# Differential attention: a score unit of the long sequence holds 1024 keys of one map instead of 512 keys of both

## The reference

```
qh = q.reshape(B, T, H, 2, HD).transpose(3, 0, 2, 1, 4) * (HD ** -0.5)
kh = k.reshape(B, T, H, 2, HD).transpose(3, 0, 2, 1, 4)
bias = -slopes[:, None, None] * jnp.abs(tq[:, None] - pos[None, :])
s = jnp.einsum('ibhqd,ibhkd->ibhqk', qblk, kh) + bias
p = jax.nn.softmax(s, axis=-1)
a = p[0] - lam * p[1]
return jnp.einsum('bhqk,bhkv->bhqv', a, vh)
```

## Time and profile before

| | |
|---|---|
| median of 3 runs | 3404.91 us (3400.65 to 3405.81) |
| profiled execution | 3406.49 us |
| its span | 3404.7 us |
| TensorE matmuls, busy | 3281.1 us (96%) |
| VectorE, busy | 1989.6 us (58%) |
| ScalarE, busy | 1324.1 us (39%) |
| GpSimd, busy | 1106.1 us (32%) |
| mean granted clock of TensorE | 0.985 |

### The profile page before, as it was taken

One profiled execution on the slowest core, in us unless ns is written; L12 is line 12 of the kernel. 1 busy time (PEld: TensorE's weight loads), 2 busy tenths in 40 slices (PEclk: granted clock), 3 DMA queues, 4 the chain that ended last, 5 costly groups with the idle time before them and its releaser, 6 DMA issues. The chain is left out here.

```text
span 3404.7 us, 50932 instructions
## 1 busy us (share of the span) xinstructions
PE 3281.1 (96%) x19032; PEld 2557.6 (75%) x19032; DVE 1989.6 (58%) x4609; ACT 1324.1 (39%) x2165; POOL 1106.1 (32%) x511
## 2 busy tenths in 40 slices
PE   7999999998999999999999988999999888999998
PEld 6888888886878888888877765666666556888887
DVE  3322312226566656665568788888888566556654
ACT  3111111114334343344323336767676555333322
POOL 3322323243333343333333325555555433000000
PEclk9999999999999999999999999999999999999999
DMA  6545445565454544544448965122221266667562
GB/s 214 182 153 188 154 156 176 173 208 177 133 182 146 180 151 125 190 145 141 131 161 292 324 210 155 45 75 64 67 62 38 100 229 229 226 230 237 176 217 75
DMA packets 317906, 554.89 MB, mean 163 GB/s; under 512 B 35421, under 2 KB 114525, under 8 KB 317662
## 3 DMA queue, kind: packets, MB, share of 16 engines
q1 hardware_dynamic: 266510, 471.26, 42.9%
q10 hardware_dynamic: 51152, 80.38, 6.5%
HBM read 382.03 MB, written 169.50 MB: 162 GB/s over the span
## 5 line engine op out<-in xcount | busy, mean ns | idle before, releaser
L731 POOL TENSOR_TENSOR glaf_w_lo<-early_raw,glaf_w_hi 128x1024 fp32r<-128x1024 f32 x140 | 350.0, 2500 | 638.6 <-ACT glaf_w_hi L705 638.6
L760 PE MATMUL glaf_dense_acc<-h_hi,glaf_w_hi 128*128 128x512 f32 x1120 | 444.0, 396 | 4.1 <-ACT glaf_dense_out L714 4.1
L760 PE MATMUL glaf_dense_acc<-h_lo,glaf_w_hi 128*128 128x512 f32 x1120 | 446.6, 399 | 0.0
L760 PE MATMUL glaf_dense_acc<-h_hi,glaf_w_lo 128*128 128x512 f32 x1120 | 437.0, 391 | 0.0
L1749 DVE CUSTOM_DVE_ANT_0 front_p<-diff_s_ps,ahead_table 128x512 f32<-128x512 f32 x544 | 347.4, 687 | 74.0 <-PE diff_s_ps L1611 73.0
L514 POOL TENSOR_TENSOR proj_w_lo<-early_raw,proj_w_hi 128x1024 fp32r<-128x1024 f32 x84 | 204.6, 2438 | 478.9 <-DVE proj_w_hi L476 478.9
L1692 ACT ACTIVATE front_p<-front_p,diff_neg_max 128x2048 f32<-128x2048 f32 (+1 forms) x160 | 278.7, 1743 | 7.0 <-DVE diff_neg_max L1757 7.0
L1635 PE MATMUL diff_oT_ps<-diff_aT,diff_v 128*128 128x512 f32 x544 | 273.3, 603 | 5.2 <-ACT diff_aT L1686 5.2
L201 PE MATMUL proj_acc<-h_hi,proj_w_hi 128*128 128x512 f32 x672 | 262.8, 391 | 0.0
L203 PE MATMUL proj_acc<-h_hi,proj_w_lo 128*128 128x512 f32 x672 | 261.6, 389 | 0.0
L202 PE MATMUL proj_acc<-h_lo,proj_w_hi 128*128 128x512 f32 x672 | 261.5, 389 | 0.0
(11 more groups left out here) (215 smaller groups left out, 7149.1 us busy)
## 6 DMA issues: line engine op xcount, KB each, us to landing
early_raw<-in_w_zg SPq DMA_DIRECT2D x180, 512.0 KB, 4.7
early_raw<-in_w_stream SPq DMA_DIRECT2D x80, 512.0 KB, 3.6
scratch_zg<-glaf_dense_out SPq DMA_DIRECT2D x140, 256.0 KB, 2.3
items_raw<-in_w_br SPq DMA_DIRECT2D x120, 256.0 KB, 2.9
merge_gate<-scratch_zg SPq DMA_DIRECT2D x120, 256.0 KB, 3.2
scratch_featT<-proj_out ACTq DMA_DIRECT2D x80, 256.0 KB, 2.2
items_br_hi<-scratch_item_hi SPq DMA_DIRECT2D x60, 256.0 KB, 5.8
items_br_lo<-scratch_item_lo SPq DMA_DIRECT2D x60, 256.0 KB, 6.7
```

Source lines behind the costliest of these rows:

```text
L731: pool.tensor_tensor(self.w_lo[:, s], self.raw[:, u % self.RAW], self.w_hi[:, s], ALU.subtract).then_inc(self.lo_split, 1)
L760: done = pe.matmul(self.acc[:, u % self.banks], a, x, start=i == 0, stop=i == self.PER - 1)
```

## The change

A unit of a long tile now holds 1024 keys of one map: unit `c` is map `c % 2`, keys 1024 (c // 2) onward. The two banks of a unit lie side by side, and VectorE reads both in one pass of 1024 columns with one slice of `table` and one maximum. `mx` shrinks from four numbers per map to two. A short tile keeps its one unit of 512 keys of both maps and its two passes. `biased` is raised once per unit instead of once per pass. TensorE waits in the first tile of a head for both key slots that a unit reads, and SP waits, before it reloads slot 0 or 1, for unit 1 of the old head's last tile, and before slot 2 or 3 for unit 3.

```diff
-        mx = m.sb("mx", [P, SLOTS, 2, TMAX // KC])
+        mx = m.sb("mx", [P, SLOTS, 2, TMAX // KC // 2])
...
+        def parts_of(T, c):
+
+            if T == KC:
+                return [(i, i, 0) for i in range(2)]
+            return [(e, c % 2, c // 2 * 2 + e) for e in range(2)]
...
-                    sp.wait_ge(scores_done, chunks_before[first_group[old + 1]] - heads[old][1] // KC + oc + 1)
+                    sp.wait_ge(scores_done, chunks_before[first_group[old + 1]] - heads[old][1] // KC + (1 if heads[old][1] == KC else oc // 2 * 2 + 2))
...
-                chunk = n.c0 + c
-                key, b = keys.index((n.head, c)), n.g % 2
+                chunk, b = n.c0 + c, n.g % 2
+                parts = [(e, i, keys.index((n.head, kc))) for e, i, kc in parts_of(n.T, c)]
...
                 if n.opens_head:
-                    pe.wait_ge(k_in[key % KS], 64 * (key // KS + 1))
+                    for key in dict.fromkeys(key for _, _, key in parts):
+                        pe.wait_ge(k_in[key % KS], 64 * (key // KS + 1))
                 if chunk >= 2:
-                    pe.wait_ge(biased, 2 * chunk - 2)
+                    pe.wait_ge(biased, chunk - 1)
...
-                for i in range(2):
-                    pe.matmul(s_ps[:, chunk % 2, i], q_high[:, b, i, cols], k[:, key % KS, i], start=True, stop=False)
-                    done = pe.matmul(s_ps[:, chunk % 2, i], q_low[:, b, i, cols], k[:, key % KS, i], start=False, stop=True)
+                for e, i, key in parts:
+                    pe.matmul(s_ps[:, chunk % 2, e], q_high[:, b, i, cols], k[:, key % KS, i], start=True, stop=False)
+                    done = pe.matmul(s_ps[:, chunk % 2, e], q_low[:, b, i, cols], k[:, key % KS, i], start=False, stop=True)
...
-                start = TMAX - P - n.tile * P + c * KC
-                for i in range(2):
-                    dve.tensor_tensor_reduce(out=p[:, n.slot, i, c * KC:(c + 1) * KC], in0=s_ps[:, (n.c0 + c) % 2, i],
-                                             in1=table[:, start:start + KC], scale=SLOPES[n.h], scalar=-3.0e38, op0=ALU.add, op1=ALU.max,
-                                             accum_out=mx[:, n.slot, i, c:c + 1]).then_inc(biased, 1)
+                spans = [(slice(0, 1), 0), (slice(1, 2), 1)] if n.T == KC else [(slice(0, 2), c % 2)]
+                for banks, i in spans:
+                    at = 0 if n.T == KC else c // 2
+                    width = KC * (banks.stop - banks.start)
+                    start = TMAX - P - n.tile * P + at * width
+                    done = dve.tensor_tensor_reduce(out=p[:, n.slot, i, at * width:(at + 1) * width],
+                                                    in0=s_ps[:, (n.c0 + c) % 2, banks].rearrange("p b k -> p (b k)"),
+                                                    in1=table[:, start:start + width], scale=SLOPES[n.h], scalar=-3.0e38, op0=ALU.add, op1=ALU.max,
+                                                    accum_out=mx[:, n.slot, i, at:at + 1])
+                done.then_inc(biased, 1)
...
-                dve.wait_ge(biased, 2 * (n.c0 + n.units))
-                dve.tensor_reduce(neg_max[:, n.slot], mx[:, n.slot, :, 0:n.units], AXX, ALU.max, negate=True).then_inc(max_ready, 1)
+                dve.wait_ge(biased, n.c0 + n.units)
+                dve.tensor_reduce(neg_max[:, n.slot], mx[:, n.slot, :, 0:max(1, n.units // 2)], AXX, ALU.max, negate=True).then_inc(max_ready, 1)
```

## The result

| | before | after |
|---|---|---|
| median of 14 runs | 3404.66 us (3398.18 to 3406.03) | 3409.06 us (3404.36 to 3413.84) |
| profiled execution, its span | 3406.49, 3404.7 us | 3411.85, 3410.0 us |
| first long score unit to first cross-attention scores | 644.12 us | 648.35 us |

The ratio is 1.0016, with a 95% interval of 1.0009 to 1.0023: 0.16% slower, under the bound of 0.2%, and not faster. Predicted were 3410.8 us and +0.17%.

What follows compares the result with a forecast made beforehand. TensorE was taken to set the pace in the long heads, with VectorE having spare time. Terms -1.3 + 0.3 + 6.9 = +5.9 us gave 3412.4 us profiled, 3410.8 us for the median (+0.17%); range 3405 to 3416 us.

Steps and rivals of the forecast that it cites:

- The key stall: At three changes between long heads, TensorE waits for keys reloaded later and needed earlier: 2.3 us each, 6.9 us in all.
- The upper bound of 2.9 us per change: Key wait at each long-head change, bounded from landing times and a long issue: 1.9 to 2.9 us, 5.7 to 8.7 altogether.
- The first long head: Its third unit now needs the last key transfer, which the fourth needed before: 0.3 us lost.
- The pass: VectorE's bias-and-maximum pass over 1024 columns: 1220 ns, holding VectorE 1.147 us, saving 0.08 us per unit, 20.5 us of VectorE's time.
- The 1313 ns that the bound and the rival rest on: Time of L1770's 1024-column form; by it a unit would lose 0.01 to 0.06 us, the wide pass not being cheaper.
- What the relief is worth: VectorE's shorter pass counts only in 44 us after the short sequence ends: 16 x 0.08 = 1.3 us gained.
- The place of the earlier trace: The 44 us at 2084 to 2128, where TensorE's score matmuls wait for VectorE's pass; 1.3 us gain expected there.
- the two mix waits: TensorE transposes waiting for VectorE in two places of the long heads, 1.6 us in 450, taken as beyond the relief's reach.
- The pass is cheaper: Judges the rival that the wide pass is not cheaper, its saving eaten: 3412.1 to 3413.1 us, chance 0.10.
- the reload isn't hidden: Judges the rival that key reloads at head changes stay hidden, with SP issuing every 0.5 us: 3404.5 us, chance 0.10.
- The last key did not land late: Judges the rival that the last key lands as late as the worst: up to +9 us, 3414 to 3420, chance 0.06.
- The clock rival: TensorE's granted clock falls to half after key waits at three head changes: +5.4 us, 3416.2 us, chance 0.08.

Runs made afterwards that it cites:

- e8: The changed kernel with keys loaded by map as units read them, but the first long head's keys still loaded by slots: 3401.55 us, ratio 0.9989.
- e3: The changed kernel with its new units and key waits, but two passes of 512 columns per unit again: 3410.79 us, ratio 1.0024.
- e4: The kernel before with only the two key waits of the changed kernel added: 3412.09 us, ratio 1.0028.
- e10: The kernel before with only the changed kernel's two key waits, run once more: 3412.48 us (one run).
- e9: The changed kernel run once more, unaltered, for a second look at the clock: 3410.17 us (one run).
- e7: The changed kernel with keys loaded by map per unit, but two passes of 512 columns per unit again: 3405.72 us, ratio 1.0005.
- e1: The changed kernel with keys loaded by map, four transfers per unit, freed and waited for by that unit; wide pass kept: 3401.01 us, ratio 0.9999.
- e2: The changed kernel with keys loaded by map per unit, one 256 KB transfer replacing two of 128 KB: 3403.29 us, ratio 0.9998.
- e5: The changed kernel with all key slots freed by the old head's last unit and awaited by the new head's first: 3444.61 us, ratio 1.0122.

## Why the prediction was right, and where its terms were off

- *The key stall, the term that decides.* Predicted 3 x 2.3 = 6.9; measured 7.56 with some 0.3 of a mix wait in it, and 7.1 by e8. The mechanism is as written: SP at the semaphore, transfers 0.64 apart, the last landing 2.8 after its start. The first change was 0.5 dearer than the others, 0.3 of it by that mix wait. Nothing took the stall back. The upper bound of 2.9 us per change has no working: 2.3 and a long issue of 0.4 make 2.7.
- *The first long head.* Predicted 0.3; the profile shows a wait of 0.50, and e3 and e4 lose 0.75 and 0.6 in that group. Too low by 0.3 to 0.4.
- *The pass.* Predicted 1.147 us for a unit and 1220 ns; measured 1.14 (2109.81 to 2110.95 in VectorE's timeline of after) and 1222. The 0.08 us from the row that reads PSUM hold. The figure of the Trainium skill, page "VectorE: DVE Perf Modes", would have given 125 ns for a joined pass and not 80; here the measurement decides. The 1313 ns that the bound and the rival rest on are the mean of 62 passes of some 1.29 us and the two held ones. VectorE's busy time from one head's first unit to the next one's fell from 128.5 to 125.8 us, by 2.7 and not by 5, and the page's total by 12.4, not 20.5: two other passes on its queue grew (L1789 from 817 to 1037 ns, L1806 from 887 to 1023), 7 us in all; why is not known.
- *What the relief is worth: the mis-sized term.* Predicted 1.3 us; measured 4.1. The place of the earlier trace rows gave 1.5, about as reckoned. The 2.1 us of the two mix waits were missed: I said that such waits are 1.6 us in 450 (the window of the earlier trace rows is 532 us long) and left them at that. They were no wait for VectorE's load. They hung on which of two engines starts first, by 0.05 us, and the wide pass turned that over at both places. The last 0.5 us are spread over the other groups.
- *The rivals.* The pass is cheaper, and the reload isn't hidden. The last key did not land late in after; e4 shows it late by 0.6 to 0.8 us, and one slow issue in e10 held it back by 1.4. The clock rival did not come in after or e9, but is real: once in e4, with some 1.7 us, and once in e7, in the very place whose clock of 1.00 the prediction held against it.

The cost and where it lies were foreseen; that the number is so near is in part luck. The distance grew by 4.2 us where 5.9 were forecast, and two errors of opposite sign stand in that: 1.1 too little cost and 2.8 too little gain. Had the relief been sized right, the forecast would have been 3408.0, with the rest of the error in the cost.

## What to carry to other kernels

When a unit of work changes shape, change the shape of what feeds it too: the same wide pass lengthens the distance by 4.2 us with keys loaded in the old shape and shortens it by 2.1 to 2.9 with loads that follow the units (e1, e2, e8; of their times only e8's is clear of before, by 0.11%), because a buffer reloaded in place has only the time from its last old use to its first new one. And look at a rare wait on an engine with time to spare before calling it noise: an outlier among 64 equal passes may be an order of two engines that the change turns over.

## What the runs showed of the hardware

- VectorE's near mix (two operands in SBUF) and GpSimd's scaling, begun within 0.06 us of each other, do not share: 1.28 and 2.21 us when VectorE is first, 2.13 and 1.12 when GpSimd is; 1.28 and 1.12 when kept apart. The Trainium skill, page "SBUF — State Buffer", section "SBUF: two separate sides", describes a pair of ports that the one to start first holds for its whole instruction. The traces agree on who is held, though 2.13 us is 0.2 less than the rest of GpSimd's 1.12 and a whole 1.28 would make.
- The two mix waits stand at the same two places in before, e3, e4, e7 and e10, which have 544 passes of 512 columns, and at neither in the six runs with the wide pass. VectorE's late starts there, and those of after, each have a transfer of kind "instruction" 0.7 to 1.4 us behind them and stand whole multiples of 128 instructions apart. That the loading of instructions causes them is likely and not shown.
- Key transfers start 0.64 us apart from one queue at 128 KB and 0.61 to 0.73 at 256 KB, but the larger ones land in 4.7 us instead of 2.8, so fewer transfers don't bring data sooner.
- TensorE's granted clock stayed at 1.00 after a wait of 2.51 us in one run (e10) and fell to half, the level of 1.2 GHz, after one of 1.98 us in another (e4) and after one of 1.49 us in a third (e7). At the one wait of 3.3 us and the three of 10 us in e5 it fell each time.
